# Hyena stage of a two-layer diffusion backbone: eight modulation tiles dealt 0, 4, 4 to three input units in place of 2, 3, 3

## The chip, the cores and the metric

The kernel runs on one core of a Trainium2 chip. The metric is the device time of one execution in microseconds. Before the change the median of three runs is 2431.44 us (2430.35 to 2433.87).

## What is computed

Two layers over 256 latent tokens of width 2048, in float32. Layer 0 has attention beside a short convolution, layer 1 a Hyena long convolution; each layer ends in a squared-ReLU MLP. Every layer is modulated by six vectors of 2048 that come from the conditioning vector:

```python
sh1, sc1, g1, sh2, sc2, g2 = jnp.split(jax.nn.silu(c) @ mod_w[l] + mod_b[l], 6, axis=-1)
# odd layer
y = hyena_mixer(modulate(x, norm_mix_g[l], sh1, sc1), od_w_in[o], ...)   # p = conv3(h @ w_in) + b; x0, x1, v = split(p)
x = x + g1 * (y @ od_w_out[o])                                           # y = x0 * long_conv(x1 * v)
x = x + g2 * ffn(modulate(x, norm_ffn_g[l], sh2, sc2), ffn_w1[l], ffn_w2[l])
```

## The kernel before

Activations stay in SBUF with channels on the partitions. Every matrix product is cut into *units* of 512 output columns, numbered through the program (`U_D` = 45 is the first one of the Hyena input). A unit has four *k-steps*, kg = 0 to 3, of 512 rows of the weight matrix. For each k-step SyncE loads 1 MB of weights into `w_raw[:, kg]` (line 410), ScalarE rounds it to fp32r as `w_hi` (`hi`, line 1453, recorded under line 1451), VectorE forms the remainder `w_lo` (`lo`, line 895), and TensorE multiplies activations by both (line 511 in the Hyena input). Here a k-step is 32 matmuls with `w_hi` and 16 with `w_lo`.

The modulation vectors are mostly not computed on TensorE. `mod_rest` holds their weights transposed; a *tile* is 128 x 1024 elements (512 KB), loaded by SyncE at line 399 and multiplied and summed along its row by VectorE in one instruction (`mod_tiles`, line 903). Eight tiles, i = 0 to 7, make one group of 512 outputs. The tiles are spread over units as filling work.

The Hyena input has twelve units: for j = 0 to 3 (512 channels each) three units, here called the x1 unit (n = 0), the v unit (n = 1) and the x0 unit (n = 2). Each j also carries one group of eight modulation tiles, `MU_D + j`, needed only when the MLP behind the Hyena stage begins. `share(n, 3, 1)` deals them: tiles 0 and 1 to the x1 unit, 2 to 4 to the v unit, 5 to 7 to the x0 unit.

VectorE's order in one unit u is written out in `body` (line 912): quarter 0 of the unit's tiles, `lo(u,2)`, the mid part, quarter 1, `lo(u,3)`, quarter 2, `lo(u+1,0)`, quarter 3, the four copies of the sums out of PSUM (`fetch`, line 935), `lo(u+1,1)`, and then the work on the sums. Of two tiles the quarters get 0, 1, 0, 1; of three 0, 1, 1, 1; of four 1, 1, 1, 1. The mid part exists only in the x1 unit (`convolved(j - 1)`, lines 1404 to 1411). The work on the sums is a three-tap convolution (lines 1269 and 1274), for the v unit also the product x1 * v, and for the x0 unit it is followed by `product(j)` (lines 1391 to 1400), the product with the filter's spectrum. Its second half waits for a filter transfer that ScalarE issues at line 1733.

TensorE uses the same four PSUM banks for all twelve units, so the first matmul of a unit waits until VectorE has copied the sums of the unit before (line 935). After k-step 1 of an x1 unit TensorE runs the inverse transform of the group before (`inverse`, line 839), which waits for the end of `product` (line 1400). After an x0 unit it runs the forward transform (line 860).

SyncE's order is one queue of its own, in `unit` (line 402). It runs one unit ahead: the load of (u, kg) waits for `lo(u-1, kg)`. The own tiles stand between: the first two behind the load of k-step 2, the next two behind the load of k-step 3, and whatever is left behind the loads of k-steps 0 and 1 of the next unit. In this stage the tiles have two buffers (`NARROW`), so the load of tile i waits at line 396 until VectorE has done tile i - 2; while it waits, every load behind it in the queue waits too:

```python
elif slots is NARROW:
    sp.wait_ge(m_steps, mu * 8 + (i - 1))
```

Of the kernel before, what the change touches and what calls it, by code (L numbers as in the profile page):

```python
# [59 lines left out]
U_ODOUT = 57  # L60
# [13 lines left out]
MU_D = 32  # L74
MU_F1 = 36


EIGHT = [(0, i) for i in range(8)]


def share(n, units, mods):

    return [(c // 8, c % 8) for c in range(n * mods * 8 // units, (n + 1) * mods * 8 // units)]


VEC = {}
# [69 lines left out]
def bass_dit_kernel(nc, x_in, ctx_in, vec_in, tab_in, fwd_in, rope_in, inv_in, small_in, fw3_in, decay_in,  # L156
                    mod_first, mod_rest, ffn_w1, ffn_w2, ev_w_in, ev_w_out, od_w_in, od_w_out, out):
    stack = ExitStack()
    with stack:  # L159
# [92 lines left out]
        NARROW = [m_raw[:, i % 2, :] for i in range(4)]  # L252
# [115 lines left out]
        def _(sp):  # L368
# [4 lines left out]
            def raw_free(u, kg):  # L373

                if kg == 3:
                    sp.wait_ge(row_full, u)
                else:
                    sp.wait_ge(raw_used, u * 3 + (kg - 2))

            def mod_tiles(tiles, slots):  # L380

                for mu, i in tiles:
                    if isinstance(mu, int) and mu == 0 and i < 4:
                        if i == 0:
                            sp.wait_ge(filt_made, 8)
                        elif i == 1:
                            for stored in k_stored[0:2]:
                                sp.wait_ge(stored, 64)
                        elif i == 2:
                            sp.wait_ge(kf_full, 16)  # L390
                        else:
                            sp.wait_ge(row_turned, START)
                    elif isinstance(mu, int) and mu == MU_F1 and i < 4:
                        sp.wait_ge(m_steps, MU_F1 * 8)
                    elif slots is NARROW:
                        sp.wait_ge(m_steps, mu * 8 + (i - 1))
                    else:
                        sp.wait_ge(m_steps, mu * 8 + (i - 3))
                    sp.dma_start(slots[i % 4], mod_rest[ds(mu * 512 + i // 2 * P, P), i % 2 * 1024:i % 2 * 1024 + 1024])\
                        .then_inc(m_landed[i % 4], 16)  # L400

            def unit(u, w, row, col, own=(), before=(), first=False, slots=WIDE, old=None, rest=2):


                for kg in range(4):
                    if first:
                        raw_free(START, kg)
                    else:
                        sp.wait_ge(lo_done, (u - 1) * 4 + (kg + 1))
                    sp.dma_start(w_raw[:, kg, :].rearrange("p (c n) -> p c n", c=4),  # L410
                                 w[ds(row + kg * 512, 512), ds(col, 512)].rearrange("(c p) n -> p c n", p=P))\
                        .then_inc(landed[kg], 16)
                    if kg < 2:
                        mod_tiles(before[rest * kg + 4:rest * kg + rest + 4], old or slots)
                    else:
                        mod_tiles(own[2 * kg - 4:2 * kg - 2], slots)

            def mods(mu, tiles=EIGHT):

                return [(mu + m, i) for m, i in tiles]  # L420
# [23 lines left out]
            def mix_mods(n):  # L444
                return mods(MU_MIX, share(n, 10, 8)) if n >= 0 else ()
# [17 lines left out]
            def mlp_mods(q, u, w_row, w2_row, mu, count, before):  # L463


                for n in range(8):
                    w, row, col = (ffn_w1, w_row, q * 2048) if n < 4 else (ffn_w2, q * 2048 + w2_row, 0)
                    unit(u + n, w, row, col + n % 4 * 512, mods(mu, share(n, 8, count)),
                         mods(mu, share(n - 1, 8, count)) if n else before)
# [5 lines left out]
            def hyena(j, before, old=NARROW):  # L475
                for n, col in enumerate((1, 2, 0)):
                    unit(j * 3 + (U_D - 3 + n), od_w_in, 0, j * 512 + (col * D_MODEL - 512),
                         mods(j + (MU_D - 1), share(n, 3, 1)),
                         mods(j + (MU_D - 1), share(n - 1, 3, 1)) if n else before, slots=NARROW, old=None if n else old)

            hyena(1, mods(MU_D - 5, share(7, 8, 5)), WIDE)
            with sp.Fori(2, 5) as j:
                hyena(j, mods(j + (MU_D - 2), share(2, 3, 1)))
            unit(U_ODOUT, od_w_out, 0, 0, (), mods(MU_F1 - 1, share(2, 3, 1)), slots=NARROW)
            with sp.Fori(1, 4) as m:
                unit(m + U_ODOUT, od_w_out, 0, m * 512)
            sp.wait_ge(b_made, 96)
# [395 lines left out]
        def _(dve):  # L883
# [28 lines left out]
            def body(u, fetched, post=None, mod=None, tiles=EIGHT, mid=None, last=False, slots=WIDE, closing=False):  # L912


                tiles = [] if mod is None else [(mod + m, i) for m, i in tiles]
                part = [tiles[len(tiles) * i // 4:len(tiles) * (i + 1) // 4] for i in range(4)]
                mod_tiles(part[0], slots)
                lo(u, 2)
                if mid:
                    mid()  # L920
                mod_tiles(part[1], slots)
                lo(u, 3)
                mod_tiles(part[2], slots)
                if not last:
                    lo(u + 1, 0)
                mod_tiles(part[3], slots)
                fetched()
                if not last and not closing:
                    lo(u + 1, 1)
                if post:  # L930
                    post()
# [16 lines left out]
            def sums(u):  # L948
                for ft in range(4):
                    fetch(u, ft, center(ft))  # L950
# [432 lines left out]
            def product(j):  # L1383

                dve.wait_ge(u_full, j * 4 + 4)
                flat = worked[:, :, :].rearrange("p f t -> p (f t)")
                for hf in range(2):
                    dve.wait_ge(k_landed[hf], j * 16 + 16)
                    kr, ki = ((kf, uT)[hf][:, i, :] for i in range(2))
                    t0, t1 = flat[:, 0:512], flat[:, 512:1024]  # L1390
                    own.done(TT(yf[:, hf, :], aux[hf][:, :], kr, ALU.mult))
                    if hf:
                        dve.wait_ge(yf_ready, j * 2 + 1)
                    a = own.done(TT(t0, aux[2 + hf][:, :], ki, ALU.mult))
                    own.done(TT(yf[:, 2 + hf, :], aux[hf][:, :], ki, ALU.mult))
                    b = own.done(TT(t1, aux[2 + hf][:, :], kr, ALU.mult))
                    own.wait(a)
                    own.done(TT(yf[:, hf, :], yf[:, hf, :], t0, ALU.subtract))
                    own.wait(b)
                    TT(yf[:, 2 + hf, :], yf[:, 2 + hf, :], t1, ALU.add).then_inc(yf_ready, 1)  # L1400

            def convolved(j):

                for ct in range(4):
                    dve.wait_ge(y_full, j * 4 + (ct // 2 * 2 + 2))
                    mark = own.done(STT(out=center(ct), in0=u_blk[:, ct, :], scalar=vec[:, ds(j * 4 + (VEC["skip"][0] + ct), 1)],
                                        in1=aux[ct // 2][:, ct % 2 * T:ct % 2 * T + T], op0=ALU.mult, op1=ALU.add))
                for ct in range(4):
                    own.wait(mark - 3 + ct)
                    TT(worked[:, ct, :], center(ct), x0_blk[:, ct, :], ALU.mult).then_inc(b_val, 1)  # L1410
                low(lambda ft: ds(j * 4 + ft, 1), j * 4 + 80)

            def hyena(j, first=False):
                for n, post in enumerate((x1_in, v_in, x0_in)):
                    body(j * 3 + (U_D + n), lambda: sums(j * 3 + (U_D + n)), lambda: post(j),
                         j + MU_D, share(n, 3, 1), slots=NARROW,
                         mid=None if n or first else (lambda: convolved(j - 1)))
                product(j)

            hyena(0, True)  # L1420
            with own.loop(3, 50, 1) as j:
                hyena(j)
# [24 lines left out]
        def _(act):  # L1447
# [77 lines left out]
            def modulate(base, items):  # L1525
                for i, (_, _, _, shift, dst, k) in enumerate(items):
                    act.wait_ge(xn_ready, base + i + 1)
                    f(dst[:, k, 0:T], summed[:, i % 4, 1:T + 1], ACT.Identity, bias=shift(k)).then_inc(nrm_hi, 1)
# [320 lines left out]
```

## Time and profile before

| | us |
|---|---|
| median of three runs | 2431.44 |
| the profiled execution | 2434.37 |
| its span, first to last instruction | 2432.6 |
| TensorE matmul busy | 2341.4 |
| VectorE busy | 1817.6 |
| ScalarE busy | 1028.9 |
| Hyena input and its transforms | about 1255 to 1615 of the span |

Busy time is a sum over instructions. The span is divided by what an engine did and by what it waited for. In the timeline a row has its start in us from the span's beginning, its length, the engine, the line of the kernel, the tiles written and read, and in brackets how long the engine was idle before it and whose work ended that idle time. SPq and ACTq are DMAs as SyncE and ScalarE issue them.

### The profile page before, as it was taken

What the parts mean: (1) busy time and instruction counts of PE and PEld (TensorE: products, weight loads), DVE (VectorE), ACT (ScalarE), POOL (GpSimd) and SP (SyncE); (2) the same over time, 40 slices, a digit from 0 to 9 for tenths busy, and PEclk for the clock granted to TensorE, in tenths of its full rate; (3) what the DMA queues carried; (4) which work ended last, traced back from release to release, by engine and by line L of the source; (5) the groups of instructions that cost most, each with busy time, mean ns of one, the idle gap of its engine ahead of it and who ended that gap; (6) DMA issues with size and microseconds to landing.
All of it is one profiled execution on the core that took longest, in us unless ns stands there. A gap on an engine that the chain in (4) does not pass through costs nothing. (4 is left out here: it accounts for less than half of the span.)

```text
span 2432.6 us, 36269 instructions
## 1 busy us (share of the span) xinstructions
PE 2341.4 (96%) x13888; PEld 2022.4 (83%) x13888; DVE 1817.6 (75%) x2409; ACT 1028.9 (42%) x1023; POOL 6.9 (0%) x7
## 2 busy tenths in 40 slices
PE   6989799989999999999989999999999999999997
PEld 2358588878888888888889999988888888888887
DVE  3567789988888888888887777866878665566565
ACT  4534533444444444444443322334444444444444
POOL 0000000000000000000000000000000000000000
PEclk7799999989999999999999999999999999999999
DMA  9997389969888888888766556455687555555552
GB/s 354 305 329 285 115 317 341 353 254 324 312 294 307 322 295 309 299 320 307 292 226 235 183 198 242 161 203 206 229 292 274 186 178 190 197 184 191 190 190 105
DMA packets 266040, 613.97 MB, mean 252 GB/s; under 512 B 12208, under 2 KB 12336, under 8 KB 265456
## 3 DMA queue, kind: packets, MB, share of 16 engines
q1 hardware_dynamic: 260992, 602.08, 69.4%
q10 hardware_dynamic: 4912, 9.96, 1.2%
q8 instruction: 100, 1.64, 0.3%
q14 instruction: 36, 0.29, 0.0%
HBM read 605.70 MB, written 6.29 MB: 252 GB/s over the span
## 5 line engine op out<-in xcount | busy, mean ns | idle before, releaser
L895 DVE TENSOR_TENSOR w_lo<-w_raw,w_hi 128x2048 fp32r<-128x2048 f32 x372 | 849.1, 2289 | 242.0 <-ACT w_hi L1451 239.2
L1451 ACT ACTIVATE w_hi<-w_raw 128x2048 fp32r<-128x2048 f32 x372 | 709.7, 1912 | 558.6 <-PE acc L568 154.3
L568 PE MATMUL acc<-act_a,w_hi 128*128 128x512 f32 x1216 | 295.2, 396 | 7.1 <-issue 4.5
L568 PE MATMUL acc<-act_b,w_hi 128*128 128x512 f32 x1216 | 290.2, 391 | 0.0
L568 PE MATMUL aux<-act_a,w_hi 128*128 128x512 f32 x1216 | 290.1, 391 | 0.0
L568 PEld LDWEIGHTS acc<-act_a,w_hi 128*128 128x128 f32 x1216 | 226.8, 191 | 53.8 <-issue 5.8
L568 PEld LDWEIGHTS acc<-act_b,w_hi 128*128 128x128 f32 x1216 | 223.5, 188 | 43.3
L568 PEld LDWEIGHTS aux<-act_a,w_hi 128*128 128x128 f32 x1216 | 223.4, 188 | 43.3
L568 PE MATMUL aux<-act_b,w_hi 128*128 128x512 f32 x1024 | 244.3, 391 | 0.0
L903 DVE SCALAR_TENSOR_TENSOR m_raw<-m_raw,wide 128x1024 f32<-128x1024 f32 x180 | 217.8, 1216 | 6.3 <-DMA m_raw<-mod_rest 6.0
L568 PEld LDWEIGHTS aux<-act_b,w_hi 128*128 128x128 f32 x1024 | 188.2, 188 | 36.4
L511 PE MATMUL acc<-act_a,w_hi 128*128 128x256 f32 x1536 | 198.4, 288 | 8.2 <-DVE summed L935 5.5
L511 PEld LDWEIGHTS acc<-act_a,w_hi 128*128 128x128 f32 x1536 | 191.7, 195 | 11.4 <-DVE summed L935 5.6
L903 DVE SCALAR_TENSOR_TENSOR scr<-scr,wide 128x1024 f32<-128x1024 f32 x140 | 169.2, 1217 | 3.8 <-DMA scr<-mod_rest 3.8
L594 PEld LDWEIGHTS acc<-act_a,w_lo 128*128 128x128 f32 x1216 | 155.9, 191 | 6.0
L594 PEld LDWEIGHTS aux<-act_a,w_lo 128*128 128x128 f32 x1216 | 155.9, 191 | 6.0
L594 PEld LDWEIGHTS acc<-act_b,w_lo 128*128 128x128 f32 x1216 | 155.9, 191 | 5.9
L594 PE MATMUL aux<-act_a,w_lo 128*128 128x256 f32 x1216 | 157.7, 283 | 0.0
L594 PE MATMUL acc<-act_b,w_lo 128*128 128x256 f32 x1216 | 157.7, 283 | 0.0
L594 PE MATMUL acc<-act_a,w_lo 128*128 128x256 f32 x1216 | 157.7, 283 | 0.0
L594 PEld LDWEIGHTS aux<-act_b,w_lo 128*128 128x128 f32 x1024 | 131.3, 191 | 4.9
L594 PE MATMUL aux<-act_b,w_lo 128*128 128x256 f32 x1024 | 132.8, 283 | 0.0
(179 smaller groups left out, 1982.2 us busy)
## 6 DMA issues: line engine op xcount, KB each, us to landing
w_raw<-ffn_w SPq DMA_DIRECT2D x256, 1024.0 KB, 7.0
m_raw<-mod_rest SPq DMA_DIRECT2D x180, 512.0 KB, 6.6
scr<-mod_rest SPq DMA_DIRECT2D x140, 512.0 KB, 7.1
w_raw<-od_w_in SPq DMA_DIRECT2D x48, 1024.0 KB, 8.1
w_raw<-ev_w_in SPq DMA_DIRECT2D x36, 1024.0 KB, 9.2
w_raw<-mod_first SPq DMA_DIRECT2D x32, 1024.0 KB, 9.4
w_raw<-ev_w_out SPq DMA_DIRECT2D x16, 1024.0 KB, 9.7
w_raw<-od_w_out SPq DMA_DIRECT2D x16, 1024.0 KB, 5.3
```

The source lines that it names most:

```text
L511: return pe.matmul(banks[ft][:, 0:T], w, rhs[:, k, a:a + T], start=start, stop=stop)
L568: return pe.matmul(banks[:, ft, :], w_hi[:, kg % 2, kc * 512 + ft * P:kc * 512 + ft * P + P], rhs[:, k, :], start=(k == 0), stop=False)
L594: mm = pe.matmul(banks[:, ft, 0:T], w_lo[:, kg % 2, kc * 512 + ft * P:kc * 512 + ft * P + P], rhs[:, k, 0:T], start=False, stop=(k == 15))
L895: TT(w_lo[:, kg % 2, :], w_raw[:, kg, :], w_hi[:, kg % 2, :].bitcast(F32), ALU.subtract)\
L903: STT(out=raw, in0=raw, scalar=1.0, in1=wide[:, i % 2 * 1024:i % 2 * 1024 + 1024], op0=ALU.mult, op1=ALU.mult, accum_out=m_part[:, i:i + 1 ...
L1451: return act.activation(out_, in_, func, **kw)
```

## The change

A new function deals the eight tiles: none to the x1 unit, tiles 0 to 3 to the v unit, 4 to 7 to the x0 unit. It takes the place of `share(n, 3, 1)` on both sides that must agree, SyncE's loads and VectorE's work, and in the two places where the last unit of a group is named as the one before.

```diff
+def hyena_share(n):
+
+    return EIGHT[(0, 0, 4)[n]:(0, 4, 8)[n]]
@@ SyncE
             def hyena(j, before, old=NARROW):
                 for n, col in enumerate((1, 2, 0)):
                     unit(j * 3 + (U_D - 3 + n), od_w_in, 0, j * 512 + (col * D_MODEL - 512),
-                         mods(j + (MU_D - 1), share(n, 3, 1)),
-                         mods(j + (MU_D - 1), share(n - 1, 3, 1)) if n else before, slots=NARROW, old=None if n else old)
+                         mods(j + (MU_D - 1), hyena_share(n)),
+                         mods(j + (MU_D - 1), hyena_share(n - 1)) if n else before, slots=NARROW, old=None if n else old)
             hyena(1, mods(MU_D - 5, share(7, 8, 5)), WIDE)
             with sp.Fori(2, 5) as j:
-                hyena(j, mods(j + (MU_D - 2), share(2, 3, 1)))
-            unit(U_ODOUT, od_w_out, 0, 0, (), mods(MU_F1 - 1, share(2, 3, 1)), slots=NARROW)
+                hyena(j, mods(j + (MU_D - 2), hyena_share(2)))
+            unit(U_ODOUT, od_w_out, 0, 0, (), mods(MU_F1 - 1, hyena_share(2)), slots=NARROW)
@@ VectorE
                     body(j * 3 + (U_D + n), lambda: sums(j * 3 + (U_D + n)), lambda: post(j),
-                         j + MU_D, share(n, 3, 1), slots=NARROW,
+                         j + MU_D, hyena_share(n), slots=NARROW,
                          mid=None if n or first else (lambda: convolved(j - 1)))
```

## Rows read from the trace of the kernel before

**Rows 1.** The page, busy us (share of the span) xinstructions, whole span.
```profile
PE 2341.4 (96%) x13888; PEld 2022.4 (83%) x13888; DVE 1817.6 (75%) x2409; ACT 1028.9 (42%) x1023; POOL 6.9 (0%) x7
```

**Rows 2.** Waits, 1250 to 1600 us: who <- whom: total us, times, longest.
```profile
PE acc L511 <- DVE summed L935: 5.5, 4, 1.9
```

**Rows 3.** Timeline, group j = 1, v unit into x0 unit, all engines.
```profile
1373.47 2.29 DVE L895 TENSOR_TENSOR w_lo<-w_raw,w_hi 128x2048 fp32r<-128x2048 f32 x1
1375.67 1.22 DVE L903 SCALAR_TENSOR_TENSOR m_raw<-m_raw,wide 128x1024 f32<-128x1024 f32 x1
...
1377.08 0.33 SPq L399 DMA_DIRECT2D m_raw<-mod_rest  x1
...
1377.71 1.74 SPq L410 DMA_DIRECT2D w_raw<-od_w_in  x3
1378.02 2.29 DVE L895 TENSOR_TENSOR w_lo<-w_raw,w_hi 128x2048 fp32r<-128x2048 f32 x1 [1.12 <-ACT w_hi L1451]
...
1381.54 2.08 PE L511 MATMUL acc<-act_a,w_lo 128*128 128x256 f32 x16
...
1385.02 1.91 ACT L1451 ACTIVATE w_hi<-w_raw 128x2048 fp32r<-128x2048 f32 x1 [7.12 <-DMA w_raw<-od_w_in]
1387.05 2.29 DVE L895 TENSOR_TENSOR w_lo<-w_raw,w_hi 128x2048 fp32r<-128x2048 f32 x1 [5.60 <-ACT w_hi L1451]
...
1389.26 1.22 DVE L903 SCALAR_TENSOR_TENSOR m_raw<-m_raw,wide 128x1024 f32<-128x1024 f32 x1
...
1390.41 1.41 DVE L935 COPY summed<-acc 128x256 f32<-128x256 f32 x4
...
1390.88 4.09 PE L511 MATMUL acc<-act_a,w_hi 128*128 128x256 f32 x32 [1.50 <-DVE summed L935]
```

**Rows 4.** Timeline, group j = 1, x0 unit into the next x1 unit.
```profile
1401.94 1.21 DVE L903 SCALAR_TENSOR_TENSOR m_raw<-m_raw,wide 128x1024 f32<-128x1024 f32 x1
...
1403.33 0.33 SPq L399 DMA_DIRECT2D m_raw<-mod_rest  x1
1404.32 1.64 SPq L410 DMA_DIRECT2D w_raw<-od_w_in  x3
...
1411.70 1.91 ACT L1451 ACTIVATE w_hi<-w_raw 128x2048 fp32r<-128x2048 f32 x1 [7.49 <-DMA w_raw<-od_w_in]
...
1417.72 1.41 DVE L935 COPY summed<-acc 128x256 f32<-128x256 f32 x4
...
1421.34 4.39 PE L511 MATMUL acc<-act_a,w_hi 128*128 128x256 f32 x32
...
1425.70 0.69 DVE L1391 TENSOR_TENSOR scr<-aux,scr 128x512 f32<-128x512 f32 x1
...
1430.22 0.69 DVE L1391 TENSOR_TENSOR scr<-aux,scr 128x512 f32<-128x512 f32 x1 [0.83 <-DMA scr<-k_freq]
```

**Rows 5.** Timeline, TensorE alone: first matmuls of the x0 unit, j = 0, 2, 3.
```profile
1304.67 4.06 PE L511 MATMUL acc<-act_a,w_hi 128*128 128x256 f32 x32 [0.52 <-DVE summed L935]
...
1477.54 5.58 PE L511 MATMUL acc<-act_a,w_hi 128*128 128x256 f32 x32 [1.87 <-DVE summed L935]
...
1564.95 4.09 PE L511 MATMUL acc<-act_a,w_hi 128*128 128x256 f32 x32 [1.66 <-DVE summed L935]
```

**Rows 6.** Timeline: inverse transforms of j = 0, 1, 3; second product halves of j = 0, 2.
```profile
1347.66 7.17 PE L839 MATMUL aux<-late,scr 128*128 128x256 f32 x32 [0.49 <-DVE scr L1400]
...
1433.95 6.31 PE L839 MATMUL aux<-late,scr 128*128 128x256 f32 x28 [0.54 <-DVE scr L1400]
...
1607.71 7.17 PE L839 MATMUL aux<-late,scr 128*128 128x256 f32 x32 [0.24 <-DVE scr L1400]
...
1343.92 0.69 DVE L1391 TENSOR_TENSOR scr<-aux,scr 128x512 f32<-128x512 f32 x1 [1.99 <-DMA scr<-k_freq]
...
1517.83 0.69 DVE L1391 TENSOR_TENSOR scr<-aux,scr 128x512 f32<-128x512 f32 x1 [3.03 <-DMA scr<-k_freq]
```

**Rows 7.** Windows: stretch, its length, busy by engine, then granted clock, DMA share, GB/s.
```profile
1476.00:1480.00 4.00, 2.46 (x16) 2.46 (x17) 4.00 (x8) 0.16 (x1) 0.00 (x0) 0.84 0.48 161
1480.00:1484.00 4.00, 4.00 (x27) 4.00 (x27) 4.00 (x11) 0.84 (x1) 0.00 (x0) 0.73 0.70 258
```

## The prediction

> **What bounds the kernel now.** I read the page first: TensorE is busy for 2341.4 us of a span of 2432.6, 96% [rows 1]. So only what opens, widens or closes a gap on TensorE can move the time, and VectorE's total work, which the change leaves as it is, says little. The second view is the list of waits over the Hyena stage. It holds one entry for TensorE that has to do with tiles: 5.5 us in 4 waits for VectorE's copies of the sums at line 935 [rows 2], once per group j. The third view is the timeline of one group, to see what stands behind that wait. The reader should follow it backwards from the gap.
>
> In group 1 TensorE is idle for 1.50 us before the first matmul of the x0 unit, which starts at 1390.88, because the copies of the v unit's sums start only at 1390.41. They stand in VectorE's order behind a tile (1389.26) and behind a `lo` at 1387.05. That `lo` is the one of k-step 0 of the x0 unit; it was 5.60 us late because ScalarE's `hi` of the same k-step started at 1385.02, and that one had waited 7.12 us for its weights [rows 3]. The weights were late because they were asked for late: SyncE issued their load at 1377.71. The `lo(v,0)` that this load formally waits for lies a whole unit back. What held SyncE is the wait at line 396: tile 4's load (1377.08) stands ahead of it and needs tile 2 done, and VectorE started tile 2 only at 1375.67 [rows 3]. So the chain that opens the gap is: tile in quarter 1 of the v unit, tile load, weight load, `hi`, `lo`, tile in quarter 3, copies, TensorE. The same gap is 0.52, 1.87 and 1.66 us in groups 0, 2 and 3 [rows 5].
>
> A second small gap stands at the inverse transform, which waits for the end of `product`: 0.49, 0.54 and 0.24 us for j = 0, 1 and 3 [rows 6].
>
> **The change part by part.** *Price of a tile on VectorE.* From the tile at 1389.26 to the copies behind it at 1390.41 are 1.15 us [rows 3]; I use 1.15 for each tile in a chain.
>
> *The x1 unit loses its two tiles.* That saves VectorE 2.3 us there, and I cost it at nothing: none of the waits of the stage has TensorE held at the x1 unit's sums or at its `lo`s; rows 2 has four waits for the copies, and rows 3 and 5 show all four at the x0 unit. Without the tiles VectorE waits that much longer for `hi` or for the last matmul. On SyncE the load of k-step 3 of the x1 unit and the first loads of the v unit are no longer held by tiles 0 and 1 and go earlier. Nothing waits for them now, so that is worth nothing by itself either.
>
> *The v unit has four tiles, one in each quarter.* Quarter 0, empty before, now holds tile 0, so `lo(v,2)` moves from 1373.47 to 1374.62. TensorE wants it at 1381.54 [rows 3], so this by itself is hidden by about 5 us. But quarter 1 moves too: its tile starts 1.15 later, at 1376.82. The question is what SyncE waits for now. Tiles 2 and 3 stand behind the load of k-step 3 of the v unit; tile 2's load needs tile 0, tile 3's needs tile 1, which is the tile of quarter 1. Behind tile 3's load comes again the load of k-step 0 of the x0 unit. So the hold is the same one, released by the tile in quarter 1, only that this tile now has another ahead of it. The load goes at 1378.86 in place of 1377.71, with 512 KB ahead of it as before, so I take the same 7.3 us from issue to `hi` (1377.71 to 1385.02, [rows 3]). `hi` starts at 1386.17, `lo` at 1388.20, tile 3 at 1390.41, the copies at 1391.56, TensorE at 1392.03. The gap is 2.65 in place of 1.50. The `lo(v,3)` in between does not give the 1.15 back: it waited 1.12 us for `hi` [rows 3] and now starts where it did, but it is not in the chain. Four groups: 4 x 1.15 = 4.6 us.
>
> *The x0 unit has four tiles too.* VectorE enters it 1.15 late like TensorE. Tile 4 in quarter 0 adds 1.15 ahead of the tile in quarter 1, so tile 5 starts 2.30 late (1401.94 to 1404.24), and so do tile 7's load, the three weight loads of the next x1 unit (1404.32 to 1406.62), `hi` (1411.70 to 1414.0), the copies (1417.72 to 1420.0) and the start of `product` (1425.70 to 1428.0) [rows 4]. TensorE does not need the copies at once: it runs the forward transform until 1421.34 [rows 4], 1422.5 with the shift. A copy that starts at 1420.0 frees its bank about 0.5 later, as in rows 3. So no third gap. Next late is the inverse transform. `product`'s first half takes 3.7 us, from 1425.70 to 1430.22 less the 0.83 of waiting, and the second half waited 0.83 us for its filter transfer. With 2.30 us of delay that wait is used up and the second half starts at about 1431.7, some 1.5 after 1430.22. The inverse transform would start that much after 1433.95, at 1435.4, while TensorE gets there at 1433.41 + 1.15 = 1434.56 [rows 4, 6].
>
> *Sum over the groups, TensorE's clock unchanged.* Offset at the inverse transform, against before: in group 0 VectorE had waited 1.99 us for the filter transfer, which swallows most of its 2.30, so TensorE sets the start: 1347.17 + 1.15 against 1347.66, +0.66. Group 1: +1.5 from above. Group 2 had a wait of 3.03 for the transfer [rows 6], which swallows it all: +1.1. Group 3 has no wait for the transfer in its timeline and no slack but the 0.24: +2.3. Sum 5.6 us.
>
> *The clock.* After the gap of 1.87 us in group 2 the 32 matmuls took 5.58 us where they take 4.06 to 4.09 after the gaps of 0.52 and 1.66 [rows 5], and the granted clock in that stretch was 0.84 and 0.73 [rows 7], a mean of the 2.4 GHz level and the 1.2 GHz one. So a stay of about 1.9 us was enough once, 1.66 not. After the change the four gaps are near 1.67, 2.65, 3.02 and 2.81. I count a slow stretch of 1.5 us in groups 1 to 3, of which group 2 pays now already. The delay from it covers part of what VectorE would have held: group 1 becomes 2.65 - 0.54 = 2.1, group 3 2.4. The forecast is 0.66 + 2.1 + 1.1 + 2.4 = 6.3 us.
>
> The Trainium skill (TensorE: Matmul & The Clock Gate, "Why this matters for your kernels") ties drops of the clock in mid-kernel to idle gaps longer than the 1.87 us after which rows 7 show one; by its rule the new gaps of 1.67 to 2.81 would stay without a drop. The row speaks against it; its result is the second case below.
>
> **The rivals.**
>
> *No new slow stretch.* TensorE comes back at 2.4 GHz after the longer gaps of groups 1 and 3. Gaps of 1.50 and 1.66 did so; longer ones without a drop are not in the trace. Then the sum is 5.6 us. If the drop in group 2 went as well, it is 1.6 less.
>
> *The gap does not widen (the other side).* Place: the weight load of k-step 0 of the x0 unit. In the changed kernel the queue is emptier around it, because k-step 3 of the v unit was loaded long before, and part of the 7.3 us from issue to `hi` may be waiting that would go with it. If the load came in 6.2 us, the 1.15 would be gone and the gap stay at 1.50. It decides from 1.15 us of shorter landing on. Against it: the new queue at that moment holds the same transfers, one tile and three loads. What stays is VectorE's 1.15 in the x0 unit, which reaches the inverse transform with about 0.3 in group 1 and 1.15 in group 3, 1.4 in all: 2432.8 us.
>
> *`product` becomes the bound everywhere.* VectorE is 2.30 us late at `product` in each group. If the filter transfer also comes late, because four weight loads now stand closely together ahead of it in place of three, none of the delay is swallowed: 4 x 2.3 = 9.2 us, 2440.6. For it: the wait of 3.03 in group 2 shows that the transfer can be late. Against it: the load of k-step 3 that competed with it now goes earlier.
>
> *The relief in the x1 unit pays.* Earlier weight loads leave the filter transfer alone, the inverse transforms no longer wait, and the landing is short as well: at most the 1.27 us of rows 6 come back, 2430.2. Faster by over 0.2% would want nearly all of the 5.5 us of rows 2 too, and nothing here removes the hold.
>
> **How the numbers follow.** The profiled execution took 2434.37 us with a span of 2432.6, 2.93 above the median of the three runs. 2434.37 + 6.3 = 2440.7 on that footing; against the median, 2431.44 + 6.3 = 2437.7. A measurement of this kernel can tell about 0.2%, 4.9 us, from no change. Chances: forecast 0.42; no new slow stretch 0.17 (2437.0); gap not widened 0.22 (2432.8); `product` bound 0.12 (2440.6); relief pays 0.07 (2430.2). The first two lie just above the bound of 2436.3, and the runs shown scatter over 3.5 us, so a third of them falls within 0.2%: slower 0.39 + 0.12, raised to 0.54, since errors of my small terms go rather upwards (a slow stretch in group 0 would add 1.5); same 0.41; faster 0.05. Range: from 2431.5, which leaves out the last case, to 2442, the `product` case with scatter.
>
> **What would show it.** In the changed kernel's timeline the tile of quarter 1 of the v unit starts 1.15 us later against TensorE's k-steps, and SyncE's three weight loads follow it. The wait of TensorE for line 935 is four entries of 1.7 to 3.0 us, 10 us in all. The clock falls after those of groups 1 to 3. The waits for the filter transfer shrink or go. The forecast is wrong if the weight load lands sooner than 6.5 us after its issue, if the queue is released by another tile than the one of quarter 1, or if TensorE waits at the start of an x1 or v unit.

## The result and the profile after

| | before | after |
|---|---|---|
| median, us | 2431.05 (6 runs) | 2441.36 (6 runs) |
| the profiled execution, us | 2434.37 | 2440.46 |
| its span, us | 2432.6 | 2438.7 |
| Hyena stage in it, first matmul of the input to the next norm's sums, us | 440.4 | 443.6 |

The ratio is 1.0037 (95% interval 1.0027 to 1.0047), so by the ratio the change costs 9 us and some, between 6.6 and 11.4; the two medians differ by 10.3. The two profiled executions differ by 6.1 us. Of that, 2.8 us stand ahead of the Hyena stage: its first matmul starts at 1257.91 in place of 1255.09, though both kernels run the same instructions up to there.

First the page, of the kernel after:

```profile
PE 2341.4 (96%) x13888; PEld 2023.1 (83%) x13888; DVE 1819.0 (75%) x2409; ACT 1029.1 (42%) x1023; POOL 6.9 (0%) x7
```

Busy time and instruction counts are those of rows 1; only the idle time has grown. The list of waits over the Hyena stage of the kernel after (who waits, for whom, total, times, longest; line 940 is line 935 of before):

```profile
PE acc L516 <- DVE summed L940: 8.4, 4, 3.5
...
PE aux L844 <- DVE scr L1405: 0.8, 1, 0.8
```

The 5.5 us of rows 2 have become 8.4. The inverse transform, with 1.27 us in rows 6, waits 0.8. The timeline of the kernel after, v unit of group 1 into the x0 unit, to be held against rows 3 (group 1 begins 3.27 us later here, by its inverse transform at 1350.93 against 1347.66):

```profile
1376.64 1.22 DVE L908 SCALAR_TENSOR_TENSOR m_raw<-m_raw,wide 128x1024 f32<-128x1024 f32 x1
...
1377.79 2.29 DVE L900 TENSOR_TENSOR w_lo<-w_raw,w_hi 128x2048 fp32r<-128x2048 f32 x1
1378.05 3.67 SPq L404 DMA_DIRECT2D m_raw<-mod_rest  x2
...
1379.99 1.22 DVE L908 SCALAR_TENSOR_TENSOR m_raw<-m_raw,wide 128x1024 f32<-128x1024 f32 x1
...
1382.01 1.64 SPq L415 DMA_DIRECT2D w_raw<-od_w_in  x3
...
1389.83 1.92 ACT L1456 ACTIVATE w_hi<-w_raw 128x2048 fp32r<-128x2048 f32 x1 [8.66 <-DMA w_raw<-od_w_in]
...
1391.87 2.29 DVE L900 TENSOR_TENSOR w_lo<-w_raw,w_hi 128x2048 fp32r<-128x2048 f32 x1 [7.15 <-ACT w_hi L1456]
...
1395.22 1.42 DVE L940 COPY summed<-acc 128x256 f32<-128x256 f32 x4
1395.70 1.52 PE L516 MATMUL acc<-act_a,w_hi 128*128 128x256 f32 x7 [3.05 <-DVE summed L940]
```

The new tile of quarter 0 stands at 1376.64. The tile of quarter 1 starts at 1379.99; with the group's offset of 3.27 taken off that is 1376.72, 1.05 later than in before. The weight loads follow 2.02 us behind it, as they did (1375.67 to 1377.71 there, 2.04). From the issue to `hi` the load takes 7.82 us where it took 7.31. So of the 1.55 us by which this gap has grown, 1.05 are the tile and 0.5 the transfer.

The gaps before the x0 units of groups 0, 2 and 3 in the same trace, TensorE alone:

```profile
1307.60 4.07 PE L516 MATMUL acc<-act_a,w_hi 128*128 128x256 f32 x32 [0.63 <-DVE summed L940]
...
1484.65 5.59 PE L516 MATMUL acc<-act_a,w_hi 128*128 128x256 f32 x32 [3.48 <-DVE summed L940]
...
1571.37 4.09 PE L516 MATMUL acc<-act_a,w_hi 128*128 128x256 f32 x32 [1.23 <-DVE summed L940]
```

And the windows behind the gaps of groups 1 and 2 (length, busy by engine, granted clock, DMA share, GB/s):

```profile
1396.00:1400.00 4.00, 4.00 (x23) 4.00 (x22) 4.00 (x7) 0.00 (x0) 0.00 (x0) 0.57 0.78 224
1484.00:1488.00 4.00, 3.35 (x16) 3.35 (x17) 4.00 (x8) 0.00 (x0) 0.00 (x0) 0.61 0.55 152
```

Against rows 5 the gap of group 0 has hardly grown (0.63 for 0.52), that of group 2 has (3.48 for 1.87), and that of group 3 is smaller (1.23 for 1.66). The granted clock fell to its 1.2 GHz level behind two gaps, against one in rows 7, and 32 matmuls took 5.59 us in place of 4.1.

The x0 unit of group 1 after, against rows 4:

```profile
1407.89 1.23 DVE L908 SCALAR_TENSOR_TENSOR m_raw<-m_raw,wide 128x1024 f32<-128x1024 f32 x1
...
1410.29 17.81 SPq L415 DMA_DIRECT2D w_raw<-od_w_in  x6
...
1417.94 1.91 ACT L1456 ACTIVATE w_hi<-w_raw 128x2048 fp32r<-128x2048 f32 x1 [7.42 <-DMA w_raw<-od_w_in]
...
1423.95 1.41 DVE L940 COPY summed<-acc 128x256 f32<-128x256 f32 x4
...
1431.94 0.69 DVE L1396 TENSOR_TENSOR scr<-aux,scr 128x512 f32<-128x512 f32 x1
```

Counted from the first matmul of the x0 unit, the tile of quarter 1 comes 12.19 us in (11.06 in before), the weight load 14.59 (13.44) and the start of `product` 36.24 (34.82). The fourth tile delays them by 1.13 to 1.42 us. The inverse transform of that group shows no gap. The reading that the slow stretch behind the first gap made TensorE later still is borne out by a second trace of this kernel (after_again, below), where the same group had no slow stretch and its inverse transform waited:

```profile
1438.22 7.17 PE L844 MATMUL aux<-late,scr 128*128 128x256 f32 x32 [1.20 <-DVE scr L1405]
```

In the three traces of the kernel after, no inverse transform waits in a group that had a slow stretch.

### The profile page after: what moved, and what is told of

The parts are those of the page before. It is cut to its first block and busy times, and to the rows that moved or that the text cites. A ratio compares the mean times of both kernels' runs of the same rounds, so it can differ in the third digit from the quotient of the medians.

```text
span 2438.7 us, 36269 instructions
## 1 busy us (share of the span) xinstructions
PE 2341.4 (96%) x13888; PEld 2023.1 (83%) x13888; DVE 1819.0 (75%) x2409; ACT 1029.1 (42%) x1023; POOL 6.9 (0%) x7
```

## The experiments

A measured ratio is that to the kernel before on the same chips, with its 95% interval.

**More traces of both kernels.** No edit.

> The kernel before once more, for a second trace. The question: the medians differ by 10.3 us, while the two profiled executions differ by 6.1 (2434.37 and 2440.46), of which 2.86 us are there before 190 us of the span, where both kernels run the same instructions, and 3.26 arise in the Hyena stage. If the start varies from execution to execution and the first trace of before was a long one in its Hyena stage, this trace has Hyena gaps before the x0 units that sum to clearly less than 5.55 us or no slow clock after the one in group 2. If the Hyena stage of before is steady, the gaps are 0.5, 1.5, 1.9, 1.7 within 0.3 each, and the excess of the medians lies elsewhere.

> The changed kernel once more, for a second trace. In the first the gaps before the x0 units were 0.63, 3.05, 3.48, 1.23 us where 1.67, 2.65, 3.02, 2.81 had been forecast, because the weight load of k-step 0 reached ScalarE 5.8, 7.8, 8.2, 6.0 us after its issue. If that landing time is chance of an execution, the four differ now and their order too; with 7.3 in each the gaps are those of the forecast and the time is 2 us longer. If it belongs to the addresses of each group, the same four come again within 0.3. Ratio to before 1.003 to 1.005 by either.

> A third trace of the kernel before, for the scatter of an execution: the landing of the weight load behind tile 4 (6.8 to 7.8 us so far) and whether TensorE's clock falls behind the gap of group 2 (once in two traces). If it falls in few, the profiled execution on which the prediction rests was 1.5 us slower than the usual one for that reason.

> A third trace of the changed kernel. Landings of 5.7 to 8.2 us so far at the same place; if they are chance, the gaps of groups 1 to 3 sum to 7 to 9 us again in another division, and the clock falls behind each gap above 3 us.

Before again: 2431.66 us, ratio 0.9995 (0.9986 to 1.0004), and 2431.96, ratio 0.9996 (0.9986 to 1.0006). After again: 2442.12, ratio 1.0036 (1.0022 to 1.0050), and 2442.97, ratio 1.0042 (1.0027 to 1.0056). What the traces hold:

| trace | gaps before the x0 units, j = 0 to 3 | sum | slow clock behind | gaps at the inverse transforms | Hyena stage |
|---|---|---|---|---|---|
| before | 0.52, 1.50, 1.87, 1.66 | 5.5 | j = 2 | 1.3 | 440.4 |
| before_again | 0.61, 1.44, 1.72, 1.02 | 4.8 | none | 0.7 | 437.2 |
| before_third | 0.53, 1.26, 1.27, 1.15 | 4.2 | none | 1.1 | 437.1 |
| after | 0.63, 3.05, 3.48, 1.23 | 8.4 | j = 1, 2 | 0.8 | 443.6 |
| after_again | 0.56, 1.90, 3.38, 2.64 | 8.5 | j = 2 (twice as long) | 1.4 | 444.4 |
| after_third | 0.61, 3.60, 3.39, 3.48 | 11.1 | j = 1, 2, 3 | 0.7 | 447.4 |

The gap of group 2 in before_again and the three grown gaps of after_third, TensorE alone:

```profile
1478.24 4.10 PE L511 MATMUL acc<-act_a,w_hi 128*128 128x256 f32 x32 [1.72 <-DVE summed L935]
```

```profile
1395.97 4.29 PE L516 MATMUL acc<-act_a,w_hi 128*128 128x256 f32 x21 [3.60 <-DVE summed L940]
...
1484.86 5.54 PE L516 MATMUL acc<-act_a,w_hi 128*128 128x256 f32 x32 [3.39 <-DVE summed L940]
...
1573.76 5.46 PE L516 MATMUL acc<-act_a,w_hi 128*128 128x256 f32 x32 [3.48 <-DVE summed L940]
```

So the trace on which the prediction rested had the longest Hyena stage of the three of that kernel, and the slow stretch of rows 7 is in it alone. The stage goes from a mean of 438.2 to one of 445.1, 6.9 us. The means of the gaps account for 4.5 of it (4.8 to 9.3), the slow stretches, 1.5 us each, for some 3 (one third of one per execution before, 2.3 after with the double one counted twice); together that is 0.6 more than the 6.9, and the split is only that exact. The start of the Hyena stage lies between 1255.1 and 1259.0 in these six traces, in both kernels, which is why two single traces may not be subtracted. The expectation for after_again was half right: groups 1 and 3 came otherwise than in the first trace, groups 0 and 2 the same to 0.1. That for after_third was too low: groups 1 to 3 sum to 10.5 us, where 7 to 9 were expected, and the clock fell behind each, as foreseen for gaps above 3 us.

**The two fourth tiles apart.**

```diff
-    return EIGHT[(0, 0, 4)[n]:(0, 4, 8)[n]]
+    return EIGHT[(0, 1, 4)[n]:(1, 4, 8)[n]]      # deal134
+    return EIGHT[(0, 1, 5)[n]:(1, 5, 8)[n]]      # deal143
```

> Tiles dealt 1, 3, 4: the v unit has its three tiles in quarters 1 to 3 as in before, only the x0 unit has four. Theory (the tile ahead of the one of quarter 1 in the v unit postpones the release of SyncE's queue): gaps before the x0 units as in before, 5.5 us in all, and +0.5 to +1.5 us from the inverse transforms, so 2431.5 to 2432.6. Rival (the later start of product by the fourth tile of the x0 unit is the main cost): the larger part of the 10 us is here, 2436 or more.

> Tiles dealt 1, 4, 3: only the v unit has four. Theory: the release of SyncE's queue is postponed by one tile, 1.15 us in each group, the gaps before the x0 units are those of the changed kernel (8 to 10 us in all), and with the slow clock behind them the time is 2436 to 2441. Rival (the x0 unit's fourth tile costs most): within 2 us of before.

deal134: 2436.22 us, ratio 1.0015 (1.0005 to 1.0024). deal143: 2437.01, ratio 1.0020 (1.0011 to 1.0029). Each costs about half of the change. The second is what the theory wanted; the first is 3.6 us above the upper end of what it allowed, just inside the time of the rival, though less than the larger part of the 10 us. The gaps of deal134 in groups 1 to 3 and of deal143 in groups 0 and 1:

```profile
1391.12 4.10 PE L516 MATMUL acc<-act_a,w_hi 128*128 128x256 f32 x32 [1.90 <-DVE summed L940]
...
1478.64 5.58 PE L516 MATMUL acc<-act_a,w_hi 128*128 128x256 f32 x32 [2.49 <-DVE summed L940]
...
1566.41 4.10 PE L516 MATMUL acc<-act_a,w_hi 128*128 128x256 f32 x32 [2.29 <-DVE summed L940]
```

```profile
1308.87 4.06 PE L516 MATMUL acc<-act_a,w_hi 128*128 128x256 f32 x32 [1.73 <-DVE summed L940]
...
1395.21 4.10 PE L516 MATMUL acc<-act_a,w_hi 128*128 128x256 f32 x32 [2.38 <-DVE summed L940]
```

deal143 has the gap of group 0 at 1.73, as forecast for the change itself (1.67). deal134 has three tiles in the v unit as before and still wider gaps there, 6.7 us in all: its weight loads took 7.7, 8.4 and 8.2 us to `hi` where before's took 6.9 to 7.8, and that is the whole growth of its gaps. So deal134 does not isolate the x0 unit's fourth tile: it also puts tile 3 in place of tile 4 ahead of that weight load. Its inverse transforms wait 1.2 us, about as much as before's (0.7 to 1.3).

**The hold of SyncE's queue taken away.** The third and fourth own tile of a unit are loaded behind the next unit's loads of k-steps 0 and 1. free233 keeps the deal of before, free044 that of the change.

```diff
                     if kg < 2:
-                        mod_tiles(before[rest * kg + 4:rest * kg + rest + 4], old or slots)
-                    else:
+                        if carry:
+                            mod_tiles(carry[kg + 2:kg + 3], slots)
+                        else:
+                            mod_tiles(before[rest * kg + 4:rest * kg + rest + 4], old or slots)
+                    elif not late:
                         mod_tiles(own[2 * kg - 4:2 * kg - 2], slots)
+                    elif kg == 2:
+                        mod_tiles(own[0:2], slots)
...
+                         late=True, carry=mods(j + (MU_D - 1), hyena_share(n - 1)) if n else carry)
```

> Tiles dealt 2, 3, 3 as in before, but in SyncE's queue the third own tile of a Hyena unit stands behind the next unit's load of k-step 0, so that this load no longer waits behind the tile of quarter 1. Theory (the hold of SyncE's queue opens the gap before the x0 unit): the four gaps of 0.5 to 1.9 us close, 5 us in all, and 2425 to 2428 us. Rival (VectorE's own work, or the transfer itself, sets the gap): the gaps stay above 1 us each and the time within 2 us of before.

> Tiles dealt 0, 4, 4 as in the changed kernel, but SyncE's queue has the tiles 2, 3, 6 and 7 behind the next unit's loads of k-steps 0 and 1, one each. Theory: with the hold gone the four-tile units cost nothing, the gaps before the x0 units close, product starts earlier too, and the time is that of the same queue with 2, 3, 3 within 2 us, so 2425 to 2429. Rival (a fourth tile in VectorE's own chain costs the time, 4 us for each unit that has one): 2434 or more.

free233: 2424.54 us, ratio 0.9964 (0.9952 to 0.9977). free044: 2424.86, ratio 0.9963 (0.9950 to 0.9977). Both are 8 us faster than before, slightly more than was expected, and the deal no longer matters. Timeline of free044, group 1, the load of k-step 0 of the x0 unit, the copies, and the unit's first matmuls:

```profile
1374.65 0.37 SPq L415 DMA_DIRECT2D w_raw<-od_w_in  x1
...
1387.24 1.86 DVE L945 COPY summed<-acc 128x256 f32<-128x256 f32 x4 [0.77 <-PE acc L521]
1388.48 3.76 PE L521 MATMUL acc<-act_a,w_hi 128*128 128x256 f32 x30
```

Now VectorE waits for TensorE at the copies and not the other way round. No gap before an x0 unit is left in either trace, and the only slow stretches are the two at the norms on either side of the stage; it takes 430.7 and 430.0 us, 7.5 and 8.2 less than the mean of before. The gaps of before (4.8 us before the x0 units, 1.0 at the inverse transforms) and its share of slow stretches (0.5) are 6.3 of that; the rest is not accounted for. VectorE executes four tiles in the v unit of free044 in the same quarters as in the changed kernel, so those tiles alone open no gap. Taking the hold away also moves a 512 KB tile from ahead of the weight load to behind it; that the hold counts is shown by the next experiment, which changes it alone. These are the best versions found, and beat both kernels.

**The same hold made longer.** In before, for j = 1 to 3, tile 4's load waits for tile 3.

```diff
-                        sp.wait_ge(m_steps, mu * 8 + (i - 1))
+                        sp.wait_ge(m_steps, mu * 8 + (i if i == 4 and not isinstance(mu, int) else i - 1))
```

> The kernel before, with one hold made longer: in the groups j = 1 to 3 tile 4's load waits for tile 3 in place of tile 2, so SyncE's queue is released by the tile of quarter 2 of the v unit, which starts 4.6 us after that of quarter 1; VectorE's work is as before. Group 0 is unchanged. Theory: each of the three gaps grows by about 4.6 us (1.5 to 6, 1.8 to 6.4, 1.4 to 6) while the gap of group 0 stays near 0.55, and with slow clock behind each the time is 2431.7 + 13.7 + up to 4.5 = 2445 to 2450. Rival (the hold is hidden and VectorE's order sets the gap): within 3 us of before.

2453.39 us, ratio 1.0084 (1.0068 to 1.0099), 20.4 us slower than before on the same chips and 3 above the upper end of what was expected. Timeline of late_release: in group 1 the tile that releases the queue, the loads, `hi`, TensorE; then TensorE in groups 2 and 3:

```profile
1382.79 1.22 DVE L903 SCALAR_TENSOR_TENSOR m_raw<-m_raw,wide 128x1024 f32<-128x1024 f32 x1
...
1384.19 0.33 SPq L399 DMA_DIRECT2D m_raw<-mod_rest  x1
1384.82 1.82 SPq L410 DMA_DIRECT2D w_raw<-od_w_in  x3
...
1392.41 1.91 ACT L1451 ACTIVATE w_hi<-w_raw 128x2048 fp32r<-128x2048 f32 x1 [11.95 <-DMA w_raw<-od_w_in]
...
1398.27 2.08 PE L511 MATMUL acc<-act_a,w_hi 128*128 128x256 f32 x8 [6.33 <-DVE summed L935]
```

```profile
1491.72 5.94 PE L511 MATMUL acc<-act_a,w_hi 128*128 128x256 f32 x32 [6.52 <-DVE summed L935]
...
1583.51 6.10 PE L511 MATMUL acc<-act_a,w_hi 128*128 128x256 f32 x32 [5.95 <-DVE summed L935]
```

The three gaps are 6.33, 6.52 and 5.95, as foretold, and group 0, left alone, has 0.46. With no change to VectorE's work the gap follows the release of the queue one for one: 4.6 us of hold, 4.9, 4.9 and 4.7 us of gap over the means of the three traces of before. A slow stretch stands behind each, twice the usual length.

**The hold taken away behind one unit only,** with the deal of the change.

```diff
+                         late=n == 1, carry=mods(j + (MU_D - 1), hyena_share(1)) if n == 2 else ())      # vfree044
+                         late=n == 2, carry=() if n or start else mods(j + (MU_D - 2), hyena_share(2)))  # x0free044
```

> Tiles dealt 0, 4, 4, the hold of SyncE's queue taken away behind the v unit only; behind the x0 unit it stays, one tile later than in before. It asks where the 4 us of the x0 unit's fourth tile (deal 1, 3, 4) come from. Theory A (they come through the gap before the next x0 unit, by longer landings and slow clock in that execution's lottery, and the inverse transform costs next to nothing): 2424.5 to 2427, no gap before an x0 unit, less than 1.5 us at the inverse transforms. Theory B (product is 2.3 us late behind the x0 unit's hold): 2428 to 2431, with gaps at the inverse transforms of 3 us and more in all.

> Tiles dealt 0, 4, 4, the hold taken away behind the x0 unit only; behind the v unit it stays as in the changed kernel. Theory A: nearly all of the change's cost stays, gaps before the x0 units of 8 to 10 us in all with slow clock behind one to three, 2438 to 2441.5. Theory B: 4 us go, 2435 to 2438.

vfree044: 2427.94 us, ratio 0.9979 (0.9970 to 0.9988). x0free044: 2437.44, ratio 1.0024 (1.0014 to 1.0035). Neither theory fits whole. vfree044 comes 0.06 us under the range of B and 0.9 over that of A, and its gaps at the inverse transforms, 2.5 us in all, lie between the two. x0free044 has the time of B and the gaps of A. These runs and free044 were measured on different chips, so they are compared by their differences to the kernel before on the same chips: free044 -8.2 us, vfree044 -4.4, x0free044 +5.1, the changed kernel +10.3. With the v unit's hold gone, the x0 unit's costs 3.8 us over free044, and the trace of vfree044 has 2.5 of them at the inverse transforms:

```profile
1348.62 7.17 PE L851 MATMUL aux<-late,scr 128*128 128x256 f32 x32 [0.50 <-DVE scr L1412]
...
1433.72 7.17 PE L851 MATMUL aux<-late,scr 128*128 128x256 f32 x32 [1.10 <-DVE scr L1412]
...
1518.64 7.17 PE L851 MATMUL aux<-late,scr 128*128 128x256 f32 x32 [0.92 <-DVE scr L1412]
```

The v unit's hold alone costs 13.3 us over free044, with gaps of 0.67, 2.32, 4.05 and 1.92 and slow clock behind the last two. Together they cost 18.5.

**The landing of the weight load.** The two tile buffers exchanged, in the changed kernel.

```diff
-        NARROW = [m_raw[:, i % 2, :] for i in range(4)]
+        NARROW = [m_raw[:, (i + 1) % 2, :] for i in range(4)]
```

> The changed kernel with the two tile buffers exchanged: even tiles in the second, odd tiles in the first. The question is a finding of the traces: the weight load of k-step 0 of group 0's x0 unit reaches ScalarE 5.7 to 5.8 us after its issue where tile 3 is loaded just ahead of it and 6.8 to 6.9 where it is tile 4, in every trace; in groups 1 to 3 it is rather the other way, 7.7 against 7.3 in the mean. If the buffer written decides, group 0 comes at 6.8 to 6.9 now and groups 1 to 3 at 7.3. If the tile's address in DRAM or the order of the queue decides, group 0 stays at 5.7 to 5.8. The time by both within 2 us of the changed kernel.

2441.37 us, ratio 1.0038 (1.0024 to 1.0052). Timeline of buffers044, group 0:

```profile
1292.99 1.53 SPq L415 DMA_DIRECT2D w_raw<-od_w_in  x3
...
1298.68 1.91 ACT L1456 ACTIVATE w_hi<-w_raw 128x2048 fp32r<-128x2048 f32 x1 [6.10 <-DMA w_raw<-od_w_in]
```

5.69 us: in group 0 the buffer is not what decides. Groups 1 to 3 came at 7.1, 6.1 and 8.2, too scattered to tell. In group 0 the difference is already there in the tile's own load: tile 3 landed 3.2 to 3.3 us after its issue in all six traces that have it there, tile 4 4.3 to 4.5 in all five. Whether that is the tile's place in DRAM or something else that comes with tile 3 in place of tile 4 was not tried and stays open.

## Why the prediction was right, and where it was off

It forecast +6.3 us, 2437.7, in a range of 2431.5 to 2442.0; measured are 2441.36 and about +9 to +10. The sign, the mechanism and the range held; the size came out too small by a third. Most of what is missing is not in the traces of the stage: there the change costs 6.9 us in the mean, 0.6 more than forecast.

*The chain that opens the gap: shown.* It was read backwards from one gap in rows 3. late_release lengthened the one link and the gap followed; free233 and free044 removed it and the gaps went.

*The release one tile later, 4 x 1.15: right.* The tile of quarter 1 came 1.05 later in group 1 and 1.14 in group 0. The step that failed is "I take the same 7.3 us from issue to `hi`". In group 0 the load took 5.78 in place of 6.83, so that group's forecast of 1.67 became 0.63. In groups 1 to 3 it took between 6.0 and 8.4. By the prediction's own sign, a landing sooner than 6.5 us, it failed in groups 0 and 3 of the first trace. The means of the three traces each give +4.5 us for the four gaps against 4.6 forecast, so the errors cancelled, which is luck.

*The x1 unit's relief worth nothing: right.* No trace of the changed kernel has TensorE waiting for tiles or copies there.

*The x0 unit's fourth tile: under-sized.* It was put down to the inverse transforms alone, where the sum without the clock had 5.6 - 4.6 = 1.0 us. deal134 costs 4.2 (1.2 to 5.8 by its interval), and keeping the x0 unit's hold 3.8 over free044. The delay at `product`, counted from the start of the x0 unit, was 1.42 us in group 1 where 1.15 had been worked out, but the gaps at the inverse transforms did not grow in the three traces, 0.7 to 1.4 us before as after. vfree044 shows why: the delay is real and worth 2.5 us of gaps as soon as the first gap is closed; beside that gap, TensorE comes late to the inverse transform anyway. What deal134 pays shows in its trace before the x0 units, in slower landings with tile 3 ahead and a slow stretch behind 2.49 us. Whether its single trace is typical is open.

*The clock: the right number of stretches, in other places, and too little counted for them.* The forecast counted one slow stretch in before and three after, two new ones. Three traces show one, none, none before and two, one of double length, and three after, which is 0.3 and 2.3 in the mean, again two new ones. But the step "of which group 2 pays now already" rested on the one execution that had it: group 2 had a stretch in one of three traces before and in all three after, while groups 1 and 3 had theirs in two and in one. The sum added only 0.7 us for the two (6.3 - 5.6), since the delay at `product` was to cover the rest. With the inverse transforms that makes 1.7 us beside the 4.6 of the gaps. The traces have 2.4 (6.9 - 4.5), none of it in waits, since those at the inverse transforms are no longer than before.

The rival "no new slow stretch" falls: every trace of the changed kernel has one or more. The prediction had set beside it the rule of the Trainium skill (TensorE: Matmul & The Clock Gate, "Why this matters for your kernels"). In the traces of the changed kernel all drops stand behind gaps of 3.05 us and more, which agrees with that rule; but gaps of 1.87 in before, 1.92 in x0free044, 2.33 in deal143 and 2.49 in deal134 brought slow stretches too, and there the measurement decides against it.

*The other rivals.* "The gap does not widen" came true in group 0, by a landing shorter by 1.05 us, and in no other group of the first trace but group 3. The reason given for it, an emptier queue, is not borne out: in deal143, with four tiles in the v unit too but tile 4 ahead of the load, group 0 took 6.9 us as in before, and in deal134, with three tiles and tile 3 ahead, 5.7. "`product` becomes the bound everywhere" did not come true: the wait for the filter transfer shrank from between 2.1 and 5.8 us in the traces of before to at most 0.5 in those of after, and the inverse transforms' gaps stayed. "The relief pays" did not either.

*What is not accounted for.* The medians differ by 10.3, the stage by 6.9 in the means of three traces each. The six profiled executions differ by 8.0 in the mean, 1.2 of it ahead of the stage. The rest, some 2.3, lies in which executions were traced: the three of before took 3.3, 1.2 and 3.6 us more than the medians of the measurements that they belong to, those of after 0.9 less, the same and 1.1 more. So the traces show before slower than it usually is, and no trace shows where the usual execution saves its time.

## What to carry to other kernels

When an engine waits for data, ask when the load was issued and what stood ahead of it in its queue: a small load that waits for its buffer holds up every large one behind it, and the release of that small load was here worth its delay one for one on TensorE. Put loads that must wait for a buffer behind the loads that needn't; two changed places in the queue brought 8 us here, where moving the filling work between units could only choose how much was lost. And take a second trace before an item of 1.5 us that comes and goes is booked as a property of the kernel.

## What the hardware showed that was not expected

- The 1 MB load of k-step 0 behind a 512 KB one took 6.0 to 8.8 us from issue to use at one and the same place of groups 1 to 3 in the eleven traces that keep the hold, 7.6 in the mean with tile 3 ahead of it and 7.3 with tile 4; in group 0 it was the other way round and steady, 5.69 to 5.83 in all six with tile 3 ahead of it and 6.76 to 6.91 in all five with tile 4.
- Before the x0 units TensorE's clock stood at its 1.2 GHz level behind every gap of 3.05 us and more, and behind none of 1.73 and less. In between it went either way: 1.87, 1.92, 2.33 and 2.49 with, 1.90 (twice), 2.29, 2.32, 2.35, 2.38 and 2.64 without.
- The same first 190 us, on the same instructions, took up to 3.6 us more in one execution than in another.
